# Expert routing in a hybrid trunk step: counts in their own bank, one rank instruction, a weight subtraction ahead of the last slot numbers

## What is computed

```python
def moe(h, w_router, b_router, w_gate, w_up, w_down):
    t = h.reshape(B * T, Dm)
    scores = jax.nn.sigmoid(jnp.einsum('nd,de->ne', t, w_router))
    sel = (scores + b_router).reshape(-1, N_EXPERT_GROUPS, EXPERTS_PER_GROUP)
    group_score = jnp.sum(lax.top_k(sel, TOP_K)[0], axis=-1)
    best = jnp.argmax(group_score, axis=-1)
    in_group = jnp.take_along_axis(sel, best[:, None, None], axis=1)[:, 0]
    _, local = lax.top_k(in_group, TOP_K)
    idx = best[:, None] * EXPERTS_PER_GROUP + local
    ...
    a = jax.nn.silu(hg) * hu * gate[..., None].astype(t.dtype)
    y = jnp.einsum('nef,efd->nd', a, w_down)
```

## Time and profile before

| | us |
|---|---|
| median of 3 runs | 1387.06 |
| lowest, highest | 1386.13, 1388.38 |
| profiled execution | 1387.46 |
| its span (first to last instruction) | 1385.7 |
| busy in it: PE, DVE, ACT | 1150.6, 801.9, 616.8 |
| experts of layer 0, first gate product to last down product | 409.1 to 708.5 |
| experts of layer 1 | 1034.8 to 1333.7 |

### The profile page before, as it was taken

The page is one execution under the profiler, slowest core; times in us unless marked ns, Lnnn a source line. Parts: engine busy times, 40 slices in busy tenths (PEclk is TensorE's granted clock), DMA queues, the critical chain, the costliest instruction groups (busy, mean ns, idle before and its releaser), DMA issues.

```text
span 1385.7 us, 14694 instructions
## 1 busy us (share of the span) xinstructions
PE 1150.6 (83%) x5476; PEld 829.7 (60%) x5476; DVE 801.9 (58%) x1064; ACT 616.8 (45%) x715; POOL 111.9 (8%) x124
## 2 busy tenths in 40 slices
PE   3499887779679999999944998789469999999942
PEld 2166444345367888888832764555267888888832
DVE  3202243431577889888835023671476888888936
ACT  1100144340227777777611003560137777777611
POOL 4000020000010101111001001100010011111000
PEclk8699989999769999999976999999759999999975
DMA  9971467771548999999739133001117999999421
GB/s 259 335 226 63 147 228 274 244 244 61 191 170 292 368 369 379 371 374 376 280 112 266 61 122 95 11 1 61 61 65 276 370 381 373 374 368 373 185 102 46
DMA packets 88270, 310.21 MB, mean 224 GB/s; under 512 B 31225, under 2 KB 35573, under 8 KB 75917
## 3 DMA queue, kind: packets, MB, share of 16 engines
q1 hardware_dynamic: 65116, 279.17, 55.4%
q0 software_dynamic: 11792, 18.65, 4.4%
q10 hardware_dynamic: 11296, 11.54, 2.5%
HBM read 307.07 MB, written 24.27 MB: 239 GB/s over the span
## 4 chain that ended last, share of the span: by engine, by line
PE 74%; DVE 10%; DMA 5%; ACT 4%; issue 4%; ACTq 2%; SPq 1%; POOL 0%; POOLq 0%; DVEq 0%
PE bank L741 15%; PE bank L976 13%; PE bank L970 12%; PE bank L971 12%; DMA ring<-in_w_ada 3%; PE bank L725 3%; ACT work L1157 3%; PE bank L848 2%; PE bank L960 2%; PE bank L748 2%; PE bank L862 2%; DVE diag L1325 2%; PE bank L950 1%; ACTq L1129 1%; PE bank L795 1%
## 5 line engine op out<-in xcount | busy, mean ns | idle before, releaser
L1610 DVE TENSOR_TENSOR ring_r<-ring,work_r 128x4096 fp32r<-128x4096 f32 x96 | 421.5, 4417 | 5.7 <-ACT work_r L1208 5.6
L1208 ACT ACTIVATE work_r<-ring 128x4096 fp32r<-128x4096 f32 x96 | 348.6, 3633 | 139.5 <-PE bank L971 118.7
L970 PE MATMUL bank<-work_r 128*128 128x512 f32 x768 | 311.4, 405 | 21.5 <-ACT work_r L1208 9.6
L971 PE MATMUL bank<-work_r 128*128 128x512 f32 x768 | 304.3, 396 | 0.0
L741 PE MATMUL bank<-hT,ring 128*128 128x384 f32 (+1 forms) x640 | 213.9, 495 | 13.5 <-DVE hT L1380 12.2
L976 PE MATMUL bank<-ring_r,work_r 128*128 128x512 f32 x768 | 195.1, 396 | 0.8 <-DVE ring_r L1610 0.8
L741 PEld LDWEIGHTS bank<-hT,ring 128*128 128x128 f32 (+1 forms) x640 | 122.4, 192 | 100.3 <-DVE hT L1380 13.9
L970 PEld LDWEIGHTS bank<-work_r 128*128 128x128 f32 x768 | 147.9, 193 | 53.2 <-issue 19.2
L976 PEld LDWEIGHTS bank<-ring_r,work_r 128*128 128x128 f32 x768 | 144.3, 188 | 35.3 <-DVE ring_r L1610 1.7
L971 PEld LDWEIGHTS bank<-work_r 128*128 128x128 f32 x768 | 147.6, 192 | 29.4
L1062 ACT ACTIVATE work<-bank 128x384 f32<-128x384 f32 (+6 forms) x79 | 37.4, 495 | 225.3 <-PE bank L741 94.0
(11 more groups left out here) (199 smaller groups left out, 1130.5 us busy)
## 6 DMA issues: line engine op xcount, KB each, us to landing
ring<-in_w_gate SPq DMA_DIRECT2D x32, 2048.0 KB, 10.0
ring<-in_w_up SPq DMA_DIRECT2D x32, 2048.0 KB, 10.4
ring<-in_w_down SPq DMA_DIRECT2D x32, 2048.0 KB, 10.5
ring<-in_w_ada SPq DMA_DIRECT2D x24, 2048.0 KB, 8.6
ring<-in_w_in SPq DMA_DIRECT2D x4, 2048.0 KB, 11.8
work<-yscr ACTq DMA_DIRECT2D x12, 512.0 KB, 6.8
ring<-in_w_out SPq DMA_DIRECT2D x4, 1280.0 KB, 7.7
ring<-in_w_in SPq DMA_DIRECT2D x12, 256.0 KB, 8.4
```

The lines of the kernel that those rows point to most:

```text
L970: mm(b[:], x_hi[:, k, :], hi[:, k, half, :], start=(k == 0), stop=False)
L971: last = mm(b[:], x_lo[:, k, :], hi[:, k, half, :], start=False, stop=False)
L1208: A_(w_hi[:, slot % 2, :], ring[slot][:], ACT.Copy).then_inc(s_hi, 1)
L1610: tt(ring_r[slot][:], ring[slot][:], w_hi[:, slot % 2, :].bitcast(F32), ALU.subtract).then_inc(s_lo, 1)
```

## The change

Three edits. The count products write to bank 7 and have a semaphore of their own, `s_counted`; the rank bank's signal is given ahead of them. The row `iota` holds 1 to 128, so that the rank needs no -1, and +1 and mask are one instruction, `stt`. In `experts` the first weight subtraction, `rest(0, 0, 0)`, stands ahead of `slots(NG - 1)`; maximum and cast of the totals, and the wait for all four groups of slot numbers, stand behind `tokens_rest(0)`.

```diff
@@ constants @@
-    put("iota", i[None, :])
+    put("iota", i[None, :] + 1)
@@ PE, rank @@
-                    mm(b[:, t * NE:(t + 1) * NE], cv("tri"), m[:, t, :], start=(t == 0), stop=True)
+                    last = mm(b[:, t * NE:(t + 1) * NE], cv("tri"), m[:, t, :], start=(t == 0), stop=True)
+                filled((l, "rank"), last)
                 for t in range(NT):
-                    last = mm(b[:, 3 * NE:4 * NE], ones, m[:, t, :], start=(t == 0), stop=(t == NT - 1))
-                filled((l, "rank"), last)
+                    last = mm(banks[7][:, 0:NE], ones, m[:, t, :], start=(t == 0), stop=(t == NT - 1))
+                last.then_inc(s_counted, 1)
@@ DVE, rank @@
                 b = take(v, (l, "rank"))
-                chain(nc.vector.tensor_reduce(cnt[:, 0:1], b[:, 3 * NE:4 * NE], AX.X, ALU.max))
-                tc(cnti[:, 0:1], cnt[:, 0:1]).then_inc(s_cnt, 1)
-                evac((l, "rank"), ts(rank, b[:, 0:NT * NE], 1.0, None, ALU.add))
+                evac((l, "rank"), stt(rank, b[:, 0:NT * NE], 1.0, R[4], ALU.add, ALU.mult))
                 for j in route[5:]:
                     ada(l, j)
                 read_out(v, (l, "rank"))
-                chain(tt(rank, rank, R[4], ALU.mult))
-                chain(ts(rank, rank, -1.0, None, ALU.add))
@@ DVE, experts @@
                     slots(NG - 2)
-                    slots(NG - 1)
-                    v.wait_ge(s_slot, NG * (n + 1))
...
                     rest(0, 0, 0)
+                    slots(NG - 1)
                     tokens_rest(0)
+                    if p == 0:
+                        v.wait_ge(s_counted, l + 1)
+                        chain(nc.vector.tensor_reduce(cnt[:, 0:1], banks[7][:, 0:NE], AX.X, ALU.max))
+                        tc(cnti[:, 0:1], cnt[:, 0:1]).then_inc(s_cnt, 1)
+                    v.wait_ge(s_slot, NG * (n + 1))
                     rest(0, 1, 1)
```

More of the change, by code:

```diff
@@ L374, in build @@
         s_mask = sem("s_mask")
+        s_counted = sem("s_counted")
         s_cnt = sem("s_cnt")
```

## The result

The changed kernel took 1378.93 us (median of 8 runs, 1376.95 to 1382.22), the kernel before in the same comparison 1386.60 (8 runs, 1383.04 to 1391.76): ratio 0.9944, 95% interval 0.9926 to 0.9963.

What follows compares the result with a forecast made beforehand. PE held 74% of the chain; its gate-product waits came from DVE's poor order. Gains 0.46 + 1.70 + 1.78 + 1.78 = 5.72 us off 1387.06 gave 1381.3, taken as 1381.5; range 1380.0 to 1384.2.

Steps and rivals of the forecast that it cites:

- (a): Layer 0, rank in one instruction: first one-hot at 390.09 instead of 390.55, gain 0.46 us.
- (b): Layer 1, rank in one instruction and no wait for the count products: gain 1.70 us.
- The bound of 0.74: Least gain in us of (b), if layer 1's 1.00 us wait on the counts was peculiar to that execution.
- (c): Both layers, first weight subtraction ahead of the last slot numbers: first gate product starts earlier, gain 1.78 us each.
- (d): Maximum and cast behind the token subtraction delay the next weight subtraction 0.35 us; 4.5 us of cover, cost 0.
- How the numbers follow: Closing step: forecast 1381.5 at 78%, own range 1380.1 to 1383.0, widened to 1380.0 and 1384.2; faster 84%.
- the low bound: Low end of the range, 1380.0 us: rise 4.7 us after both starts, worth 0.5, and the earlier runs' spread.
- rival 1: Clock's rise behind the first gate products stays at the same moment: gain 3.06 us, 1384.0; chance 12%.
- kept on average: Clock check is free-running, so the mean distance from first gate product to rise stays and the gain is kept.
- 2: Rival: something else releases the first gate product, (c) gives nothing, 2.16 us remain, 1384.9; chance 6%.
- 3: Rival: the long DVE subtraction blocks GpSimd's token gathers, 3.7 us late in layer 0, 2.5 in layer 1, 1393.3; chance 4%.

Runs made afterwards that it cites:

- e12: The changed kernel plus five dense unused products in PE's wait ahead of the first gate product; 1375.3 +- 1.0 us, ratio 0.9925.
- e5: The changed kernel, upper-part products first for experts 0 and 1, expert 1's first weight subtraction in DVE's idle time; with e14 1375.5 +- 1.4 us.
- e14: The same kernel as e5, run again for its size; together with e5 1375.5 +- 1.4 us (12 times).

## Why the prediction missed

Its parts, in its own order:

(a) Right: 0.46 forecast, 0.47 measured in two traces (24.20 to 23.72 and 23.73, rank only).

(b) Right, and in full: 1.71. The bound of 0.74, for the case that the wait on the counts was peculiar to one execution, was not needed; the wait is in the layer 1 of every trace without the rank part.

(c) Right: 1.73 and 1.71 instead of 1.78. It is ACT that ends last now, and L1217 to PE is the hand-over that the earlier trace rows showed.

(d) Right. Maximum and cast (404.27 to 404.62) delay the second weight subtraction by 0.3 us, and PE did not wait for it.

The sum of the places was 5.72 and is 5.64. Two other steps failed, both in "How the numbers follow": the baseline with its spread, and the clock, which the sum put at nothing.

*The clock.* The prediction let the rise follow the start, and put the alternative below (the rise stays put, 3.06 us of gain). It kept the other direction for the low bound only and sized it 0.5. In layer 1 the rise did follow the start and kept its 4.7 us. In layer 0 it came 4.8 us behind the start instead of 5.9, and the expert products became 0.6 us shorter (299.56 to 298.93 on the mean of four). So the size was right and the place was wrong: it belonged in the sum. 5.64 + 0.63 makes 6.3, beside a measured 7.0 +- 0.8; the 0.7 that are left are within that interval. Against rival 1 the prediction also said that nothing ahead of the start changes the clock. e12 refutes this: five products ahead of the start moved the rise by more than 3 us. The Trainium skill (TensorE: Matmul & The Clock Gate, Part 1: The HAM clock gate) was cited for the rise shifting from run to run; in these traces its distance from the start repeats to 0.3 us in every kernel but the pair e5 and e14, so as a reason for "kept on average" the citation did not hold here. The trace had the hint: the clock came at 5.8 and 4.7 us in two places whose instructions are the same.

*The baseline and its spread.* 1387.06 was the median of three runs that lay within 2.2 us; 119 times have a mean of 1385.8 and lie within 12.7. 1.2 of the 2.7 us between the forecast of 1381.5 and the mean of 1378.8 are this, the largest single part. The low end of the range, 1380.0, lay 1.5 us under the forecast, 0.5 of it for the clock and 1.0 for the spread; the clock (0.6) and the baseline (1.2) alone exceed that.

Of the rivals, 1 and 2 are out: the rise moved with the start or by more, and PE still starts 0.10 us behind the end of DVE's token subtraction (404.36 to 404.46). 3 is out as well, with every gather at its old distance. The third gather, no longer beside the big subtraction, went from 3.08 to 0.99 us, which goes with the rule of the Trainium skill (SBUF — State Buffer, Who interferes with whom); thirteen others never took longer than 1.02 beside it, and no run here tests it. It was never waited for.

## What to carry over

When an engine idles ahead of a short urgent job, look for a long job of its queue that can be done in that idle time; the gain is then read from the next releaser, here ACT, and came out to 0.1 us at its place. A head start of one or two microseconds in front of a rising clock is worth more or less than its size, so look at the distance from start to rise in every trace, at every place where the clock is low, and try dense unused products in the wait where they hold up nothing. Do not take the spread of three runs for the spread of the kernel.

## What was unexpected of the hardware

The distance from the first gate product to the rise of the clock is the same to 0.3 us in four traces of one kernel, though the product itself starts anywhere within 4 us, and it differs between kernels from 1.3 to 6.1 us; only e5 and e14, one kernel, differ from each other by more. PE's wait of 1.67 us is followed by a dip of 3.4 us at half clock in one order of the work (rank only) and by none in another (the change). Five unused products in a wait brought the rise more than 3 us forward, and half of what that won was lost again at the next half-clock place, nearly 290 us later.
